# The conditioning product of a two-block network: from 14 matmuls a unit on TensorE to a weighting on GpSimd, spread over the first phase

## The reference, cut to what matters

```python
def second_block(x, c, norm_g, w_ada, b_ada, ...):
    B, S, D = x.shape                      # 1, 256, 1024
    for l in range(DEPTH):                 # DEPTH is 1
        mod = c @ w_ada[l] + b_ada[l]      # [1024] @ [1024, 3072]
        shift, scale, gate = jnp.split(mod, 3, axis=-1)
        ...
```

## Time and profile before

| | |
|---|---|
| median of three runs | 2061.57 us (2053.02 to 2062.0) |
| span of the profiled execution, first to last instruction | 2050.6 us |
| TensorE busy | 1910.0 us, 93% |
| VectorE busy | 547.4 us, 27% |
| ScalarE busy | 232.2 us, 11% |
| GpSimd busy | 45.1 us, 2% |
| mean granted TensorE clock | 0.962 |

### The profile page before, as it was taken

The page is one execution under the profiler, slowest core; times in us unless marked ns, Lnnn a source line. Parts: engine busy times, 40 slices in busy tenths (PEclk is TensorE's granted clock), DMA queues, the critical chain, the costliest instruction groups (busy, mean ns, idle before and its releaser), DMA issues. The chain is left out here.

```text
span 2050.6 us, 22746 instructions
## 1 busy us (share of the span) xinstructions
PE 1910.0 (93%) x9553; PEld 1199.0 (58%) x9553; DVE 547.4 (27%) x1027; ACT 232.2 (11%) x348; POOL 45.1 (2%) x39
## 2 busy tenths in 40 slices
PE   6999998999889999999999999999999977999997
PEld 5688885788765444444444444444444436667983
DVE  1642577444234210111111011011111121014412
ACT  0223122000010000000000000000000012011101
POOL 1000000211010000000000000000000000000000
PEclk9999999899688899999999999999999998999998
DMA  7343233421126599999999999999999975452240
GB/s 246 124 164 124 103 124 119 169 83 43 42 105 208 187 417 417 419 417 417 419 418 417 418 419 417 417 419 417 418 418 418 417 274 181 146 164 82 98 150 35
DMA packets 134011, 537.75 MB, mean 262 GB/s; under 512 B 5730, under 2 KB 13196, under 8 KB 101032
## 3 DMA queue, kind: packets, MB, share of 16 engines
q1 hardware_dynamic: 128880, 527.58, 65.3%
q10 hardware_dynamic: 3464, 4.85, 0.9%
q0 software_dynamic: 1616, 4.58, 0.7%
HBM read 531.23 MB, written 5.77 MB: 262 GB/s over the span
## 5 line engine op out<-in xcount | busy, mean ns | idle before, releaser
L1055 PE MATMUL small<-arena 128*64 128x512 f32 x2048 | 455.1, 596 | 12.6 <-DMA arena<-in_expert_w_gu 11.7
L1055 PEld LDWEIGHTS small<-arena 128*64 128x64 f32 x2048 | 166.2, 137 | 294.6 <-issue 253.9
L621 PE MATMUL proj<-arena 128*128 128x256 f32 x1248 | 281.3, 387 | 10.1 <-DMA arena<-in_w_in_first 6.3
L621 PEld LDWEIGHTS proj<-arena 128*128 128x128 f32 x1248 | 241.6, 195 | 45.6 <-issue 11.7
L1085 PE MATMUL small<-arena 128*64 128x512 f32 x1024 | 226.8, 594 | 24.9 <-issue 24.9
L1903 DVE TENSOR_SCALAR arena<-small 128x512 f32<-128x512 f32 x32 | 22.1, 692 | 753.2 <-PE small L1062 753.2
L1106 PE MATMUL proj<-arena 128*128 128x256 f32 x768 | 169.2, 381 | 5.1 <-DVE arena L1936 5.1
L1085 PEld LDWEIGHTS small<-arena 128*64 128x64 f32 x1024 | 84.8, 137 | 146.4 <-issue 146.4
L1106 PEld LDWEIGHTS proj<-arena 128*128 128x128 f32 x768 | 146.3, 191 | 26.2 <-DVE arena L1936 5.5
L1027 PE MATMUL small<-arena 128*128 128x64 f32 x1056 | 125.0, 278 | 0.0
L1027 PEld LDWEIGHTS small<-arena 128*128 128x128 f32 x1056 | 123.8, 196 | 1.4 <-DVE arena L1877 1.4
(11 more groups left out here) (434 smaller groups left out, 1487.4 us busy)
## 6 DMA issues: line engine op xcount, KB each, us to landing
arena<-in_expert_w_gu SPq DMA_DIRECT2D x128, 2048.0 KB, 23.9
arena<-in_expert_w_down SPq DMA_DIRECT2D x64, 2048.0 KB, 20.6
arena<-in_w_in_first SPq DMA_DIRECT2D x21, 2048.0 KB, 7.7
arena<-in_w_in SPq DMA_DIRECT2D x16, 2048.0 KB, 9.3
arena<-in_w_ada SPq DMA_DIRECT2D x6, 2048.0 KB, 7.9
arena<-in_w_branch SPq DMA_DIRECT2D x4, 2048.0 KB, 7.6
arena<-in_w_out SPq DMA_DIRECT2D x4, 2048.0 KB, 7.9
bias_rows<-arena ACTq DMA_DIRECT2D x1, 4608.0 KB
```

The source lines that it names most:

```text
L621: mm = pe.matmul(ps[:, m * T:m * T + T], w[:, k, (2 * b + m) * P:(2 * b + m + 1) * P], XT[:, k, :], start=k == 0, stop=k == KD - 1)
L1055: mm = pe.matmul(bank[CAP * half:CAP * half + CAP, :], XG[:, k, :], w[:, k % 2, n * D + half * W:n * D + half * W + W], start=k == 0, stop ...
```

## The change

The layout of the "ada" units changes: partition p now holds the eight input rows 8p to 8p+7, and `CV` holds the matching eight numbers of `c_2` on each partition. GpSimd waits until the unit is in the ring, multiplies it in place by `CV`, and folds eight blocks into one with three additions (8 to 4, 4 to 2, 2 to 1). TensorE then needs only 4 matmuls against a column of ones, which sum over partitions. VectorE copies the four columns into `MODT` and adds the bias once for all six. `ada_rows`, `CB`, `SEL` and the row buffers go.

The six units move forward in `UNITS`, into the first phase, and TensorE's six `ada` calls stand between the two halves of units C v, B f, G D 0 and G C 1 and after the fills of levels 0 and 4 of branch B. The wait for the constants moves ahead of C v.

```diff
-UNITS = (["D xr", "D gate", "C q", "C k", "C if", "C v", "C o", "B q", "B f", "B i", "B g",
-          "G D 0", "G D 1", "Wb D", "A r", "A k", "A v", "A x",
-          "G C 0", "G C 1", "ada 0", "ada 1", "ada 2", "ada 3", "Wb C", "G B 0", "G B 1", "Wb B", "G A 0", "G A 1", "Wb A", "out 0", "out 1", "ada 4", "ada 5",
+UNITS = (["D xr", "D gate", "C q", "C k", "ada 0", "C if", "C v", "C o", "ada 1", "B q", "B f", "B i", "ada 2", "B g",
+          "G D 0", "G D 1", "ada 3", "Wb D", "A r", "ada 4", "A k", "A v", "A x", "ada 5",
+          "G C 0", "G C 1", "Wb C", "G B 0", "G B 1", "Wb B", "G A 0", "G A 1", "Wb A", "out 0", "out 1",
           "ple 0", "ple 1", "pp"])
...
-                return ins["w_ada_2"][0, :, half * W:half * W + W].rearrange("(k p) n -> p k n", p=P), (KD, W)
+                return ins["w_ada_2"][0, :, half * W:half * W + W].rearrange("(p k) n -> p k n", k=KD), (KD, W)
...
+            pool.dma_start(CV, ins["c_2"][0].rearrange("(p k) -> p k", k=KD)).then_inc(sig("cond_loaded"), 16)
+            chained = [0]
+
+            def then(ins_):
+
+                chained[0] += 1
+                ins_.then_inc(sig("pool_chain"), 1)
+                pool.wait_ge(sig("pool_chain"), chained[0])
+
+            def weigh(i):
+
+                n = unit_no(f"ada {i}")
+                w = weights(f"ada {i}")
+                pool.wait_ge(sig(f"unit_in_{n % 3}"), 16 * (n // 3 + 1))
+                then(pool.tensor_tensor(w, w, over(CV, W), ALU.mult))
+                then(pool.tensor_tensor(w[:, 0:4], w[:, 0:4], w[:, 4:8], ALU.add))
+                then(pool.tensor_tensor(w[:, 0:2], w[:, 0:2], w[:, 2:4], ALU.add))
+                pool.tensor_tensor(w[:, 0], w[:, 0], w[:, 1], ALU.add).then_inc(sig("ada_weighed"), 1)
+
+            pool.wait_ge(sig("cond_loaded"), 16)
+            for i in range(4):
+                weigh(i)
             pool.wait_ge(sig("merged"), 1)
...
+            weigh(4)
+            weigh(5)
             for l in range(6):
...
+            def ada(i):
+
+                pe.wait_ge(sig("ada_weighed"), i + 1)
+                ps = small(f"ada {i}")
+                for m in range(4):
+                    mm = pe.matmul(ps[:, m:m + 1], weights(f"ada {i}")[:, 0, m * P:m * P + P], c("ones", 0, 1), start=True, stop=True)
+                mm.then_inc(sig("small_full"), 1)
...
-            ones_tokens("C v")
+            pe.wait_ge(sig("const_loaded"), 16)
+            ones_tokens("C v", 0)
             ones_channels("C o")
             ones_channels("B q")
-            pe.wait_ge(sig("const_loaded"), 16)
...
-            ones_channels("B f")
+            ones_channels("B f", between=1)
...
-            ones_channels("G D 0")
+            ones_channels("G D 0", between=2)
...
+                if l in (0, 4):
+                    ada(3 + l // 4)
...
-            ones_channels("G C 1")
...
+            ones_channels("G C 1", between=5)
...
-            ada_rows(4)
-            ada_rows(5)
-            ada(4)
-            ada(5)
-
-            pe.wait_ge(sig("small_out"), small_no("ada 5") + 1)
+
+            pe.wait_ge(sig("ada_done"), 1)
...
+            def ada(i):
+
+                do(dve.tensor_copy(MODT[:, 4 * i:4 * i + 4], full(f"ada {i}")[:, 0:4]), "small_out")
...
-            do(dve.tensor_copy(CB, over(PV2[:, 0:8], 32)))
-            do(dve.tensor_reduce(SEL, ident.rearrange("p (a b) -> p a b", b=32)[:, :, 0], AX.X, ALU.add), "cond_ready")
...
+            ada(5)
+            do(TTn(MODT, MODT, PV2[:, 16:40], ALU.add), "ada_done")
```

More of the change, by code:

```diff
@@ L39, in _place @@
     for name, n in (("ident", 128), ("headsum", 128), ("level", 7 * 128), ("strict64", 128), ("upper64", 128),
-                    ("upper", 128), ("strict", 128), ("ones", 256), ("flip", 128), ("slot", 64), ("reset64", 256),
+                    ("upper", 128), ("strict", 128), ("ones", 256), ("slot", 64), ("reset64", 256),
                     ("poolcnt", 1024), ("headrow", 1024)):
@@ L130 @@
          + ["D gx 0", "D gx 1", "D ga 0", "D ga 1"]
-         + ["C row 0", "C row 1", "C col"] + [f"C S {h}" for h in range(4)]
-         + ["C num 0", "C num 1", "C den", "C yT 0", "C yT 1"]
+         + ["ada 0", "C row 0", "C row 1", "C col", "ada 1"] + [f"C S {h}" for h in range(4)]
+         + ["C num 0", "C num 1", "C den", "ada 2", "C yT 0", "C yT 1"]
          + [f"Wb D {i}" for i in range(4)]
-         + ["B diag 0", "B diag 1"] + [f"B level {l} {j}" for l in range(7) for j in range(2)] + ["B cross"]
+         + ["B diag 0", "B diag 1"] + [x for l in range(7) for x in [f"B level {l} {j}" for j in range(2)] + ([f"ada {3 + l // 4}"] if l in (0, 4) else [])] + ["B cross"]
          + ["B o 0", "B o 1", "vectors2"]
          + ["A w 0", "A w 1", "A a 0", "A a 1", "A g 0", "A g 1", "A kk 0", "A kk 1", "B yT 0", "B yT 1"]
-         + ["A V 0", "A V 1", "ada rows 0", "A bonus 0", "A bonus 1", "ada 0", "ada rows 1"]
-         + [f"A {n} {i}" for n in ("At", "Bt", "Kt") for i in range(2)] + ["ada 1", "ada rows 2"]
-         + [f"A NT {i}" for i in range(4)] + ["ada 2", "ada rows 3"] + [f"A X0 {i}" for i in range(4)] + ["ada 3"]
+         + ["A V 0", "A V 1", "ada 5", "A bonus 0", "A bonus 1"]
+         + [f"A {n} {i}" for n in ("At", "Bt", "Kt") for i in range(2)]
+         + [f"A NT {i}" for i in range(4)] + [f"A X0 {i}" for i in range(4)]
          + [f"Wb C {i}" for i in range(4)]
@@ L148 @@
          + [f"Wb A {i}" for i in range(4)] + [f"mix {i}" for i in range(4)]
-         + ["bias", "ada rows 4", "ada rows 5", "ada 4", "ada 5", "gate8"] + [f"x1 {i}" for i in range(4)] + ["gateB 0", "gateB 1"]
+         + ["bias", "gate8"] + [f"x1 {i}" for i in range(4)] + ["gateB 0", "gateB 1"]
          + ["logits", "pT", "ple 0", "ple 1", "gateT", "rank", "ple 2", "ple 3"] + [f"pp {i}" for i in range(4)]
@@ L609, in small, with ones_channels @@
                 return small_bank[n % 4]
-            def ones_channels(what, banks=(0, 1)):
+            def ones_channels(what, banks=(0, 1), between=None):
                 w = unit(what)
                 for b in banks:
+                    if b == 1 and between is not None:
+                        ada(between)
                     name = f"{what} {b}" if not what.startswith("G") else f"{what[:-1]}{int(what[-1]) * 2 + b}"
@@ L623, in ones_channels, with ones_tokens @@
                     mm.then_inc(sig("proj_full"), 1)
-            def ones_tokens(what):
+            def ones_tokens(what, between=None):
                 w = unit(what)
                 for j in range(TT):
+                    if j == 1 and between is not None:
+                        ada(between)
                     ps = proj(f"{what} {j}")
@@ L828, in _ @@
                 to_tokens(name, src)
-            ada(1)
-            ada_rows(2)
             def head(v, h, lo, hi):
@@ L852, in _ @@
             pairs("NT", bA, kkA)
-            ada(2)
-            ada_rows(3)
             pe.wait_ge(sig("NTm_ready"), 1)
@@ L860, in _ @@
                 mm.then_inc(sig("small_full"), 1)
-            ada(3)
             merge("C")
@@ L1533, in _ @@
             do(STT(qk[:, 4:8], qk[:, 4:8], float(P) ** -0.5, cz[:, 4:8, 0:T], ALU.mult, ALU.mult), "C_qk")
+            ada(0)
             for i in range(2):
@@ L1550, in _ @@
             dve.nop().then_inc(sig("C_dist"), 1)
+            ada(1)
             dve.wait_ge(sig("C_w"), 1)
@@ L1559, in _ @@
             do(dve.tensor_copy(denC, full("C den")[:, 0:8]), "small_out")
+            ada(2)
             dve.wait_ge(sig("C_em"), 1)
@@ L1637, in _ @@
                     add_level(l - 1)
+                if l in (1, 5):
+                    ada(3 + l // 4)
                 if l > 1:
```

23 lines of the change are left out of this document (2 added, 21 removed).

## The result

The changed kernel takes 2086.9 us (median of four runs, 2085.2 to 2087.7) beside 2061.8 us of the kernel before on the same chip: ratio 1.0137, 95% interval 1.0109 to 1.0166. It is slower, by 25 us. The kernel before spreads over 15 us from run to run and the changed one over 5, so this distance moves with the sample: the same kernel, run again later, had 1.0154 (2087.5 us beside 2055.3). The profiled execution has a span of 2084.9 us, 34.3 us more than before, at a mean granted TensorE clock of 0.951 instead of 0.962. (A unit took 12 matmuls in the kernel before, 8 and 4, not the 14 of the title.)

What follows compares the result with a forecast made beforehand. First phase bound by TensorE, 340 to 380 us by VectorE's chain. -8.6 + 5.2 + 4.2 = +0.8, plus 42.7 of turns, is +43.5 on 2050.6: 2094, or 2105 us against the median; range 2057 to 2118.

Steps and rivals of the forecast that it cites:

- turns: VectorE with both operands in SBUF and a reading GpSimd alternate by whole instructions: 42.7 us, 2088 to 2118, chance 0.55.
- free running: Rival: GpSimd and VectorE do not hinder each other in the weightings; +0.8 us, 2062 us, chance 0.22.
- the clock's 7.5 us: TensorE's slower clock after three long stalls, 2.5 us added for each.
- Gains: Work removed from VectorE's chain and ahead of merge C (4.7 us) and of x1's transposes (3.9 us): 8.6 us.
- `ada` calls: Five of TensorE's six new calls stand where TensorE is the bound, 1.05 us each: 5.2 us.
- Ring: Units landing late behind freed ada slots: C o 0.9, G D 1 0.9, A k 2.4, together 4.2 us.
- Weighting 0: At 53.5 to 74 us, branch D's convolution on VectorE is held and TensorE's D product waits: 10.0 us.
- Weightings 1 to 3: From 110, 153 and 203 us, beside C rows, an idle VectorE and B's scans: 0 to 1, nothing, 1.3 us.
- Weighting 4: From 252 us, VectorE slips about 15.6 us in branch B's levels; less slack and A k's 2.4, 9.4 us.
- Weighting 5: From 293 us, VectorE's instructions ahead of `B o` slip, and `B o` on TensorE with them: 14 us.
- The sum's base: Forecast added to the profiled execution's 2050.6 us span, then 11.0 us to the median of 2061.6 us.
- shared: Rival: both engines slow down while they overlap, not in whole-instruction alternation; 10 to 25 us more, 2078 us, chance 0.13.

Runs made afterwards that it cites:

- the kernel with an idle GpSimd: The changed kernel with the four GpSimd instructions of each weighting left out, GpSimd only waiting and signalling: 2060.0 us, ratio 1.0016 to the kernel before.
- the memset kernel: The changed kernel with each weighting replaced by four GpSimd memsets of the whole unit, which only write: 2060.7 us, ratio 1.0019 to the kernel before.
- the sliced kernel: The changed kernel with each weighting cut into fifteen GpSimd instructions of 512 columns in place of four: 2064.6 us, ratio 1.0041 to the kernel before.
- late and whole: The changed kernel with weightings moved to 430 to 575 us in their four whole instructions, TensorE's calls moved too: 2056.1 us, ratio 0.999 to the kernel before.

## Why the prediction was right, and where its sizes were off

The sign, the mechanism and the places were right: turns, taken by whole instructions, at D_conv, in the levels and ahead of `B o`. The 2105 us was 18 us too high, and the range of turns, 2088 to 2118, misses 2087 at its low end. The wider one, from 2057, holds it only because it reaches down for free running, which is refuted: that much is luck. Nor does the 2088 follow from the terms named for it: 2105 less the clock's 7.5 us is 2097.5. TensorE's waits, announced as some 10 us each at the D product, at a level and at `B o`, were 6.5, 3.6 and 9.9 us.

One reading was wrong without harm. The two longest waits up to 330 us in the kernel before are not the 3.8 us ones but 6.3 and 6.0 us, for the first weights and for x; the change touches neither.

How far TensorE is behind the kernel before, read off the starts of the same instructions in the timelines, gives the bill. The fifth column is the same for the kernel with an idle GpSimd, the last the difference of the two, that is what GpSimd's instructions cost up to there:

| TensorE at | before, us | after, us | behind, us | behind with idle GpSimd, us | turns, us |
|---|---|---|---|---|---|
| gate product of D | 64.66 | 71.75 | 7.1 | 0.3 | 6.8 |
| C k | 68.11 | 78.14 | 10.0 | 0.3 | 9.7 |
| C v | 89.02 | 100.48 | 11.5 | 2.0 | 9.5 |
| C o | 102.86 | 116.58 | 13.7 | 4.2 | 9.5 |
| level 0 of B | 231.90 | 249.12 | 17.2 | 5.7 | 11.6 |
| A k | 253.75 | 276.03 | 22.3 | 9.3 | 12.9 |
| level 3 | 260.66 | 288.18 | 27.5 | 12.1 | 15.4 |
| level 4 | 269.35 | 298.63 | 29.3 | 12.1 | 17.2 |
| cross term of B | 295.43 | 327.00 | 31.6 | 13.0 | 18.5 |
| B o | 297.39 | 338.09 | 40.7 | 13.0 | 27.7 |
| G C 0 | 300.14 | 343.34 | 43.2 | 13.0 | 30.2 |
| merge C | 379.87 | 417.00 | 37.1 | 9.7 | 27.4 |
| transposes of x1 | 647.78 | 680.80 | 33.0 | 5.6 | 27.4 |

**Gains, 8.6 forecast, 9.0 measured.** From the end of L1708 (L1712 in the changed kernel) to merge C there were 20.4 us, now 15.4: 5.0 for my 4.7. From x1's end to its transposes there were 4.1 us, now nothing, 4.0 for my 3.9:

```profile
679.45 1.29 DVE L1796 SCALAR_TENSOR_TENSOR arena<-arena 128x1024 f32<-128x1024 f32 x1 [1.87 <-ACT arena L1281]
...
680.80 3.46 PE L968 MATMUL small<-arena 128*128 128x128 f32 x15 [5.54 <-DVE arena L1796]
```

**`ada` calls, 5.2 forecast, 4.1 measured** (0.95 us for the eight records of a call, 0.8 of it net, five times).

**Ring, 4.2 forecast, 7.3 measured.** C o 1.2 and G D 1 1.0 for 0.9 each; A k 3.7 for 2.4. And one that I missed, C v, 1.4: ada 0 holds one of the three slots, so C v is issued only when C k is used, and the 7 us of C if are shorter than its transfer. I had looked at the units behind a freed `ada` slot and not at the one that an `ada` unit pushes out. In sum: 4.1 + 7.3 - 9.0 = 2.4 us without GpSimd, for my 0.8. The kernel with an idle GpSimd is 5.6 us behind at x1's transposes. Part of the rest is a cost that I put at nothing, the clock behind a wait for the ring: after A k's 3.6 us its fill takes 9.87 us instead of 7.07. That the medians gave only 1.7 us comes from the kernel before, whose median lies above its profiled execution (see below).

**Turns, 42.7 forecast, 30.2 in the traces at G C 0 and 27.4 from merge C on.** Weighting 0: 10.0 plus 2.5 for the clock forecast, 9.7 measured, of which 2.9 is the D product at the lower clock. The held time of VectorE is 13.6 us (12.29 + 2.31 + 2.48 less 1.53, 0.41 and 1.53), not 17.1. Weightings 1 to 3: 1.8 forecast, 3.2 by the table; but 1.7 of it is G D 0's first half, 8.84 us for 7.15 at a granted clock of 0.81, and the memset kernel has that too (8.72 us) without a turn. Weighting 4: 11.9 forecast, 4.2 by the table (3.6 of wait and 1.8 of slow clock behind it, less 1.3, since the fill behind A k's wait ran slower still with an idle GpSimd). VectorE was held 13.8 us there, not 15.6. Of these, 3.7 were its slack, 1.0 it would otherwise have waited for TensorE ahead of the differences, and some 5.5 TensorE was late by itself (3.7 waiting for A k, 1.5 in the slow fill behind it), which leaves the wait of 3.6 us at level 3; I had deducted 3.8 and 2.4. Weighting 5: 16.5 forecast; 1.4 at the cross term, 9.1 at `B o`, 2.5 at its half clock, 13.0.

Two terms were mis-sized. One is the rate of the multiply: I took the earlier trace rows's 2.2 ns for two full operands, 9.0 us, as the only row there was, and an operand that repeats one element 512 times makes it 7.0 us at its shortest and 7.2 on the mean. Each long turn is 1.9 us shorter for it. The other is what weighting 4's turn could hide in, 10.2 us where I deducted 6.2. The 2.8 us that come back between G C 0 and merge C, where VectorE's chain is the bound, no run explains.

**The sum's base.** In the span the forecast was +43.5, and +34.3 came; that is half of the miss. The other half is the 11.0 us that I put between the profiled execution and the median. The changed kernel's median lies 2.0 us above its profiled span. The kernel before has a spread that the changed one lacks: over the 73 runs of it beside the experiments the time goes with the granted clock, 2050.9 to 2051.2 us at 0.963, 2052.6 to 2053.6 at 0.960, 2060.3 to 2064.2 at 0.956, 2065.8 to 2065.9 at 0.953. The profiled execution, at 0.962, lies at the low end of that; the changed kernel's eight runs all have 0.950 to 0.953. A distance to the median is thus no constant that a change leaves alone. In which stretch the clock is lost when it is lost stays open.

**The rivals.** Free side by side (0.22) and shared (0.13) fall with the 12.29 us of three instructions, shared also with the sliced kernel. Faster (0.05) lacked its condition: the ring's waits stood, and grew. GpSimd twice as slow on repeated elements (0.05) is refuted by the 7.2 us; it is quicker on them.

**The clock.** My 2.5 us a stall stood up: 2.9 at L701 (6.55 us for 3.62), 1.5 + 1.8 in the levels, 2.5 at `B o`. The 1.5 follows A k's wait, though, and is no price of a turn. The granted clock in three windows, from the end of the idle stretch to the refill (us, busy us and records of each engine, clock, DMA share, GB/s), is half of full speed, 1.2 GHz, while `B o` runs, and 0.96 behind it:

```profile
326.00:337.00 11.00, 1.16 (x8) 0.97 (x8) 10.65 (x8) 0.40 (x1) 9.44 (x4) 0.69 0.54 191
337.00:343.20 6.20, 5.11 (x24) 5.14 (x25) 3.31 (x6) 2.12 (x3) 0.00 (x0) 0.50 0.01 3
343.20:351.00 7.80, 7.80 (x37) 6.86 (x37) 3.31 (x4) 3.24 (x5) 0.00 (x0) 0.96 0.00 0
```

## What to carry to other kernels

An idle engine is not free room. Before work goes to GpSimd, read for its whole stretch what VectorE runs there: instructions with an operand from PSUM kept their time in every trace here (0.69 us for 512 columns), those with both operands in SBUF, and TENSOR_SCALAR from SBUF, waited for the whole GpSimd instruction, and each such wait is paid by whoever waits for VectorE. If they must overlap, cut GpSimd's instructions short enough that the held time fits in VectorE's lead (27 us became 5 here), or better, put them where VectorE works from PSUM (late and whole, the time was 2056 us). And price such a wait where it ends: 13.8 us of held time at the levels cost some 4, since TensorE was late there anyway.

## What was not expected of the hardware

- GpSimd's tensor_tensor is quicker with a repeated-element operand: 7.0 us for 4096 columns (1.7 ns an element) against 4.5 us for 2048 with two full operands (2.2 ns), as a multiply (L587) and as an addition alike. Its tensor_scalar, reading one operand only, is slower than both: 10.54 us for 4096 columns at its shortest (2.6 ns).
- A memset of 4096 columns on GpSimd takes 3.51 us, leaves VectorE's two-operand instructions alone (1.52 us for three), and holds its TENSOR_SCALAR (2.45 us for 0.41).
- The size of VectorE's instruction has no part in it: one of 4 x 256 elements beside weighting 1 took 7.06 us, while GpSimd's multiply took 7.38:

```profile
122.47 7.38 POOL L565 TENSOR_TENSOR arena<-arena 128x4096 f32<-128x4096 f32 x1 [52.20 <-DMA arena<-in_w_ada]
123.06 7.06 DVE L1536 TENSOR_TENSOR arena<-arena 4x256 f32<-4x256 f32 x1
```

- GpSimd waits in its turn: beside branch B's scans the additions of weighting 3 took 5.38 and 3.21 us for 4.5 and 2.3. It had the time.
